# The last two tiles of the second block: values first, gates by halves of the tokens, each half with a norm and store of its own

## The reference

```
gate = sigmoid(h @ w_ple_gate)        # 1024 -> 1024
h    = h + gate * (p @ w_ple_proj)    # 256  -> 1024, per-layer embedding
y    = h * rsqrt(mean(h*h, axis=-1) + 1e-6) * g_final
return y                              # 512 x 1024, f32
```

## Time and profile before

| | us |
|---|---|
| three timed runs | 2205.54, 2205.90, 2208.24 |
| median | 2205.9 |
| the profiled execution | 2205.49 |
| its span in the trace | 2203.5 |
| mean granted clock of PE, share of full speed | 0.993 |

### The profile page before, as it was taken

How to read it: one execution, slowest core, us unless ns; L and a number is a source line. 1 busy time by engine, 2 the same in 40 slices (tenths; PEclk the granted TensorE clock), 3 DMA queues, 4 the chain that set the end, 5 groups by cost and what they waited for, 6 DMA issues and landing times.

```text
span 2203.5 us, 33251 instructions
## 1 busy us (share of the span) xinstructions
PE 2167.4 (98%) x13078; PEld 1830.8 (83%) x13078; DVE 1099.0 (50%) x1711; ACT 822.7 (37%) x1397; POOL 890.8 (40%) x404
## 2 busy tenths in 40 slices
PE   8999999999999999999999999999999999999997
PEld 7987799999999867888888878888878788887876
DVE  5568655642642276540143369656664554443224
ACT  3348734313433375442233322244433332222233
POOL 2322643433443454444444433333334444444443
PEclk9999999999999999999999999999999999999999
DMA  5620045324343701333333374233223243332331
GB/s 147 171 65 2 2 131 155 89 77 129 93 127 93 204 6 39 88 94 95 95 96 90 91 170 140 83 94 84 82 81 96 77 115 95 95 95 82 93 93 67
DMA packets 374985, 210.59 MB, mean 96 GB/s; under 512 B 26399, under 2 KB 367488, under 8 KB 373968
## 3 DMA queue, kind: packets, MB, share of 16 engines
q1 hardware_dynamic: 364454, 191.94, 30.8%
q10 hardware_dynamic: 10410, 16.94, 2.8%
HBM read 196.82 MB, written 15.40 MB: 96 GB/s over the span
## 4 chain that ended last, share of the span: by engine, by line
issue 45%; PE 31%; POOL 21%; DVE 1%; ACT 1%; POOLq 0%; DMA 0%; ACTq 0%; DVEq 0%
POOL w_lo L836 20%; PE acc L974 7%; PE acc L975 7%; PE acc L976 7%; PE acc L1059 2%; PE ops L1100 2%; PE tps L1084 2%; PE ops L1098 1%; PE ops L1082 1%; PE tps L1034 0%; DVE probs L2271 0%; POOL probs L865 0%; POOLq L835 0%; PE acc L1127 0%; ACT sq_x L1698 0%
## 5 line engine op out<-in xcount | busy, mean ns | idle before, releaser
L836 POOL TENSOR_TENSOR w_lo<-raw,w_hi 128x1024 fp32r<-128x1024 f32 x328 | 799.5, 2438 | 1172.7 <-ACT w_hi L1503 1162.9
L1503 ACT ACTIVATE w_hi<-raw 128x1024 fp32r<-128x1024 f32 x327 | 346.3, 1059 | 1039.5 <-PE acc L976 1027.9
L974 PE MATMUL acc<-hr_hi,w_hi 128*128 128x512 f32 x1120 | 447.3, 399 | 1.2 <-DVE qkv L2875 0.6
L976 PE MATMUL acc<-hr_hi,w_lo 128*128 128x512 f32 x1120 | 443.0, 396 | 0.0
L975 PE MATMUL acc<-hr_lo,w_hi 128*128 128x512 f32 x1120 | 442.9, 395 | 0.0
L974 PE MATMUL acc<-hn_hi,w_hi 128*128 128x264 f32 (+1 forms) x872 | 257.7, 295 | 5.3 <-DVE hn_lo L2357 5.1
L974 PEld LDWEIGHTS acc<-hr_hi,w_hi 128*128 128x128 f32 x1120 | 210.5, 188 | 54.4 <-issue 3.7
L975 PE MATMUL acc<-hn_lo,w_hi 128*128 128x264 f32 (+1 forms) x872 | 254.1, 291 | 0.0
L976 PE MATMUL acc<-hn_hi,w_lo 128*128 128x264 f32 (+1 forms) x872 | 254.0, 291 | 0.0
L976 PEld LDWEIGHTS acc<-hr_hi,w_lo 128*128 128x128 f32 x1120 | 210.4, 188 | 50.8
L975 PEld LDWEIGHTS acc<-hr_lo,w_hi 128*128 128x128 f32 x1120 | 210.5, 188 | 49.9 <-issue 0.7
(11 more groups left out here) (435 smaller groups left out, 3689.7 us busy)
## 6 DMA issues: line engine op xcount, KB each, us to landing
raw<-in_w_up SPq DMA_DIRECT2D x64, 512.0 KB, 4.0
raw<-in_w_down SPq DMA_DIRECT2D x64, 512.0 KB, 4.1
raw<-in_w_in SPq DMA_DIRECT2D x56, 512.0 KB, 3.9
raw<-in_w_ffn_gate SPq DMA_DIRECT2D x22, 512.0 KB, 3.8
raw<-in_w_ffn_up SPq DMA_DIRECT2D x22, 512.0 KB, 3.7
raw<-in_w_in_even SPq DMA_DIRECT2D x18, 512.0 KB, 5.8
raw<-in_w_ffn_down SPq DMA_DIRECT2D x16, 512.0 KB, 4.1
raw<-in_w_in_odd SPq DMA_DIRECT2D x10, 512.0 KB, 5.6
```

What stands on the lines that cost most here:

```text
L836: nc.gpsimd.tensor_tensor(w_lo[:, part], raw[:, slot], w_hi[:, part].bitcast(F32), ALU.subtract).then_inc(sems["lo"], T.up("lo"))
L974: mm(out, w_hi[:, part, w0 + k, :], xh, start=s0, stop=False)
L976: ins = mm(out, w_lo[:, part, w0 + k, :], xh, start=False, stop=s1)
L1503: fn(w_hi[:, n % 2], raw[:, n % 4], ACT.Copy).then_inc(sems["hi"], T.up("hi"))
```

## The change

`ple` keeps three steps (tiles 0 to 5). Two new projections follow: `ple_values` (one unit of values for tiles 6 and 7, which ACT copies into `hid_2`) and `ple_gates` (two units, tiles 6 and 7). The gates are run by hand as four pieces of 24 matmuls with 256 tokens each, in the order (tile 6, tokens 0 to 255), then the transposes of tiles 4 and 5, (tile 7, first half), (tile 6, second half), then transposes and norm sums of the first half, (tile 7, second half), and the same for the second half. The halves lie in different PSUM banks.

```
     ple = Projection("ple", [...],
-                     DT // 2, DT // 2, peel=1, order=list(range(0, DT, 2)))
+                     DT // 2 - 1, DT // 2 - 1, peel=1, order=list(range(0, DT - 2, 2)))
+    ple_values = Projection("ple_values", [[(w_ple_proj, 0, 0, 2, "p", w_ple_proj[:, :, P:])], []], 1, 1, order=[DT - 2])
+    ple_gates = Projection("ple_gates", [[(w_ple_gate, 0, 0, 8, "hn2")], [(w_ple_gate, P, 0, 8, "hn2")]], 1, 1,
+                           order=[DT - 2])
+        TOKENS = SEQ // 2
+        def tokens(n):
+            return slice(TOKENS * n, TOKENS * n + TOKENS)
 # SP
             units(ple)
+            units(ple_values)
+            units(ple_gates)
 # PE
+            project(ple_values)
+            gates = []
+            def gate_half(x, n):
+                if n == 0:
+                    gates.append((next_weights(), open_()))
+                part, b = gates[x]
+                for k in range(DT):
+                    ins = three(acc[b][:, n, 0:TOKENS], part, k, hr_hi[:, k, tokens(n)], hr_lo[:, k, tokens(n)],
+                                k == 0, k == DT - 1)
+                ins.then_inc(sems["gate_full"], T.up("gate_full"))
+            def turn_last(n):
+                T.saw("result_last", 2)
+                pe.wait_ge(sems["result_last"], T.at("result_last"))
+                transposes("t_", [...4 blocks of out_t, tiles 6 and 7, two rows of tokens...])
+                T.saw("last_square", 2)
+                pe.wait_ge(sems["last_square"], T.at("last_square"))
+                b = open_("o_")
+                for q in range(2):
+                    c = slice(P * (2 * n + q), P * (2 * n + q) + P)
+                    for i, x in enumerate((sumsq, sq[:, 0, :], sq[:, 1, :])):
+                        ins = mm(ops_[b][:, q:q + 1], x[:, c], ones[:, 0:1], start=i == 0, stop=i == 2)
+                close(ins, b, "o_")
+            gate_half(0, 0)
+            turn_result(DT - 4)
+            turn_result(DT - 3)
+            gate_half(1, 0)
+            gate_half(0, 1)
+            T.saw("sumsq", DT - 1)
             pe.wait_ge(sems["sumsq"], T.at("sumsq"))
+            turn_last(0)
+            gate_half(1, 1)
+            turn_last(1)
 # ACT
             project(ple, embed, own=(0, 1))
+            def keep_values(m, s, t, b):
+                act.wait_ge(sems[f"full{b}"], T.at(f"full{b}"))
+                if t:
+                    next_hi(False)
+                fn(hid_2[:, 1, t, :], acc2[b], ACT.Copy).then_inc(sems[f"stored{b}"], T.up(f"stored{b}"))
+            project(ple_values, keep_values, own=(0, 1))
+            def gate_half(x, n): ...       # Sigmoid, 256 tokens, into hid_2
+            def squares_of_last(x, n): ... # waits "gated", Square, 256 tokens, into sq
+            def root(n): ...               # waits the sums, Sqrt of 2 columns into rstd_tok
+            def store_even(n):
+                q = 2 * n
+                T.saw("rstd_tok")
+                act.wait_ge(sems["rstd_tok"], T.at("rstd_tok"))
+                done = out_sb[:, q, 0:6 * P]
+                fn(done, done, ACT.Copy, scale=rstd_tok[:, q:q + 1]).then_inc(sems["out_act"], T.up("out_act"))
+                act.wait_ge(sems["out_act"], T.at("out_act"))
+                T.saw("out_part")
+                act.wait_ge(sems["out_part"], T.at("out_part"))
+                dma(out[q * P:(q + 1) * P, :], out_sb[:, q, :], "done")
+            gate_half(0, 0)
+            gate_half(1, 0)
+            squares_of_last(0, 0)
+            squares_of_last(1, 0)
+            gate_half(0, 1)
+            fn(small[:, 6:7], eps, ACT.Sqrt).then_inc(sems["metas"], T.up("metas"))
+            root(0)
+            fn(small[:, 7:8], eps, ACT.Sigmoid).then_inc(sems["metas"], T.up("metas"))
+            gate_half(1, 1)
+            fn(small[:, 5:6], eps, ACT.Sqrt).then_inc(sems["metas"], T.up("metas"))
+            store_even(0)
+            squares_of_last(0, 1)
+            squares_of_last(1, 1)
+            root(1)
+            store_even(1)
 # DVE
             project(ple, embed, own=(0, 1))
+            project(ple_values, lambda *_: None, own=(0, 1))
+            keep_result(DT - 4)
+            keep_result(DT - 3)
+            def gate_half(x, n): ...  # values * gate, h + that, times the gain into out_t; 256 tokens each
+            def scale_rows(n): ...    # reciprocal of 2 columns; the 256 new columns of both rows of
+                                      # tokens scaled out of PSUM; the other 768 columns of the odd row
+            gate_half(0, 0)
+            gate_half(1, 0)
+            gate_half(0, 1)
+            scale_rows(0)
+            gate_half(1, 1)
+            scale_rows(1)
```

More of the change, by code:

```diff
@@ L1465, in _ @@
             project(ple, None, H_LO, after_tile=ple_tile)
-            turn_result(DT - 2)
-            turn_result(DT - 1)
-            T.saw("sumsq", DT + 1)
+            project(ple_values)
[11 more added lines that the diff above has]
+                pe.wait_ge(sems["result_last"], T.at("result_last"))
+                transposes("t_", [(lambda t, q=q, x=x: t[:, 256 * q + P * x:256 * q + P * x + P],
+                                   out_t[:, DT - 2 + x, P * (2 * n + q):P * (2 * n + q) + P], 0)
+                                  for q in range(2) for x in range(2)])
+                T.saw("last_square", 2)
[12 more added lines that the diff above has]
+            T.saw("sumsq", DT - 1)
             pe.wait_ge(sems["sumsq"], T.at("sumsq"))
[L1470 to L1473, removed]
+            turn_last(0)
+            gate_half(1, 1)
+            turn_last(1)
         @block.scalar
@@ new lines, in _, with gate_half, squares_of_last @@
+            project(ple_values, keep_values, own=(0, 1))
+            banks = [take(T, "") for _ in range(2)]
+            def gate_half(x, n):
+                T.saw("gate_full")
+                act.wait_ge(sems["gate_full"], T.at("gate_full"))
+                fn(hid_2[:, x, 2, tokens(n)], acc[banks[x]][:, n, 0:TOKENS], ACT.Sigmoid).then_inc(
+                    sems["gate"], T.up("gate"))
+            def squares_of_last(x, n):
+                T.saw("gated")
+                act.wait_ge(sems["gated"], T.at("gated"))
+                if n == 0:
+                    act.wait_ge(sems["sumsq"], T.at("sumsq"))
+                fn(sq[:, x, tokens(n)], h[:, DT - 2 + x, tokens(n)], ACT.Square).then_inc(
+                    sems["last_square"], T.up("last_square"))
@@ new lines, in root @@
+            def root(n):
+                b = result(T, "o_")
+                act.wait_ge(sems[f"o_full{b}"], T.at(f"o_full{b}"))
+                fn(rstd_tok[:, 2 * n:2 * n + 2], ops_[b][:, 0:2], ACT.Sqrt, bias=eps, scale=1.0 / D_MODEL).then_inc(
+                    sems[f"o_stored{b}"], T.up(f"o_stored{b}"))
+            def store_even(n):
[4 more added lines that the diff above has]
+                fn(done, done, ACT.Copy, scale=rstd_tok[:, q:q + 1]).then_inc(sems["out_act"], T.up("out_act"))
@@ new lines, in _, with gate_half @@
+            keep_result(DT - 4)
+            keep_result(DT - 3)
+            def gate_half(x, n):
+                T.saw("gate")
+                dve.wait_ge(sems["gate"], T.at("gate"))
+                G, hm, k = hid_2[:, 1, x, tokens(n)], h[:, DT - 2 + x, tokens(n)], DT - 2 + x
+                step(v.tensor_tensor(G, G, hid_2[:, x, 2, tokens(n)], ALU.mult))
+                v.tensor_tensor(hm, hm, G, ALU.add).then_inc(sems["gated"], T.up("gated"))
+                dve.wait_ge(sems["gated"], T.at("gated"))
+                v.tensor_scalar(out_t[:, k, tokens(n)], hm, gains[:, 56 + k:57 + k], None, ALU.mult).then_inc(
+                    sems["result_last"], T.up("result_last"))
@@ new lines, in scale_rows @@
+            def scale_rows(n):
+                o, b = others(T, "o_"), result(T, "t_")
+                dve.wait_ge(sems[f"o_stored{o}"], T.at(f"o_stored{o}"))
+                x = rstd_tok[:, 2 * n:2 * n + 2]
+                v.reciprocal(x, x).then_inc(sems["rstd_tok"], T.up("rstd_tok"))
+                dve.wait_ge(sems["rstd_tok"], T.at("rstd_tok"))
+                dve.wait_ge(sems[f"t_full{b}"], T.at(f"t_full{b}"))
+                q = 2 * n
+                v.tensor_scalar(out_sb[:, q, 6 * P:], tps[b][:, 0:256], rstd_tok[:, q:q + 1], None, ALU.mult).then_inc(
+                    sems["out_part"], T.up("out_part"))
+                q += 1
+                v.tensor_scalar(out_sb[:, q, 6 * P:], tps[b][:, 256:512], rstd_tok[:, q:q + 1], None, ALU.mult).then_inc(
+                    sems[f"t_stored{b}"], T.up(f"t_stored{b}"))
+                done = out_sb[:, q, 0:6 * P]
+                v.tensor_scalar(done, done, rstd_tok[:, q:q + 1], None, ALU.mult).then_inc(
+                    sems["out_dve"], T.up("out_dve"))
```

44 lines of the change are left out of this document (8 added, 36 removed).

## The result

| | before | after |
|---|---|---|
| median, us | 2205.85 (11 runs, 2200.95 to 2209.56) | 2212.04 (11 runs, 2207.01 to 2217.95) |
| the profiled execution | 2205.49 | 2212.02 |
| its span in the trace | 2203.5 | 2210.0 |
| ratio to before, 95% interval | | 1.0031 [1.0019, 1.0043] |

The changed kernel is slower by 0.31%, 6.2 us in the medians, where 2213.0 was predicted. The same kernel run once more in a later comparison gave 2212.18 against 2204.39, ratio 1.0031 [1.0017, 1.0045].

A forecast was written before the change was run, and what follows sets the result against it. The prediction took PE, busy 98% of the span, to bound the kernel, with a serial tail behind it. Against the profiled 2205.5, 5.1 + 1.9 + 2.5 - 2.0 = +7.5 gave 2213.0 us, range 2209.5 to 2217.

The forecast's parts named there:

- sign of being wrong: PE's gap ahead of the first 256-column matmul under 2 us, or last gate starting within 3 us of last values' old place.
- The wait: PE, between values 6/7 and the first gate: idle for late-rounded weights and the accumulator, 5.1 us.
- The part put down to the accumulator: PE ahead of values 7: waits until DVE frees the accumulator of values 5, 1.0 us.
- The clock: First gates after PE's gap: the granted clock falls for about 3.9 us, costing +1.9, bounds 0 and some 9.
- the clock holds: Rival at the first gates: no clock fall through the gap, 2213.0 - 1.9 = 2211.1; chance 0.18.
- It falls again between the gates: Rival: a second clock fall at the transposes and one-column sums there slows the last 24 matmuls and 12 passes; 2216.0, chance 0.12.
- The norm between the gates: PE ahead of the last gate piece: the first half's transposes and one-column sums add +2.5 us.
- The tail: After the last product: sigmoid, table load, squares, sums, scaling and store take 12.1 against 14.2, so -2.0 us.
- The order on ACT: In the tail: scaling and storing the first half before the second half's squares costs some 2.8 us.
- Drain at a table change: Rival on ACT: each table change also drains it by another load's length, 1.28 in the tail; 2214.3, chance 0.04.
- Halves of a gate: PE's gates: 96 matmuls of 256 columns instead of 48 of 512, no cost, with 0.3 us either way.
- Not slower: weights in time: Rival at ACT's list after tile 4's gain: early rounding avoids stall and clock fall; 2206.0, chance 0.08.

The follow-up runs named there:

- e1: The changed kernel with ACT rounding the weights of tile 6's gate before tile 5's square and gain; ratio to before 1.0013.
- e2: The changed kernel with 16 unneeded matmuls of 512 columns filling PE's gap ahead of the first gate piece; ratio to before 1.0022.
- e3: The changed kernel with ACT taking the second half's squares before scaling and storing the first half's even rows; ratio to before 1.0033.
- e6: The changed kernel with both ACT reorderings, those of e1 and e3; ratio to before 1.0007.
- e5: The changed kernel with all four gate pieces ahead of both norms, one table load, second half's squares before the first half's store; ratio to before 1.0019.
- e7: The changed kernel with values of tiles 4 to 7 as one unit of weights, then four gate pieces, both norms last; ratio to before 0.9996.
- e9: The kernel of e7 with ACT's rounding of the next unit also moved ahead of tile 3's duty; 2201.58 against 2204.39, ratio 0.9986.
- e8: The changed kernel with e1's earlier rounding and e5's norms behind all gate pieces; ratio to before 1.0001.
- e4: The changed kernel with values still first, but whole gates of 512 tokens and one norm as before; 2214.74, ratio to before 1.0048.

## Why the prediction was right, step by step

The verdict, the mechanism and the time (2213.0, measured 2212.04) hold. By terms, with the first trace's own sizes, +7.5 was forecast and +5.9 came from values 6 to the end. That the time is nearer than the terms is luck: 0.6 of the 6.5 in that trace is the earlier offset, which nothing in the forecast stands for. Neither sign of being wrong came: the gap was 3.71 and not under 2, and the last piece of gate starts at 2195.57, 7.6 after before's values of tile 7 (2187.97).

- **The wait, 5.1: 5.0.** Every date was late by the 0.6 of the earlier offset, and otherwise in place: rounding forecast at 2178.75, seen at 2179.34; `w_lo` at 2182.4, PE's start at 2182.86. e1 moves that one instruction and takes 2.4 away. The part put down to the accumulator, 1.0, was 1.05 counted in slots (2176.44 to 2177.49), 0.81 by the bracket.
- **The clock, 1.9: 1.6**, and 2.4 in the second trace. That it would fall was right, and e2 shows the gap as its cause; it came inside the gap in one trace and 0.8 after it in the other. Of the rivals, *the clock holds* is out in both. *It falls again between the gates* is out too: 1.00 through that norm in every trace that has one there (after twice, e1, e2, e3, e6). What none of the cases held is that it can fall again in the tail alone: 1.2 us in the second trace, e1 and e2, 0 in the first trace and e3.
- **The norm between the gates, 2.5: 1.7** (2193.88 to 2195.57). A pass of one column was taken at 0.17, from 8 passes in 1.35. But those passes of before ran partly at the lower level, as the stretch of before around them shows, with a granted clock of 0.72 (it wasn't read for the prediction). At the full clock a pass is 0.11.

```profile
2193.90:2195.30 1.40, 1.33 (x8) 1.25 (x8) 1.15 (x2) 0.02 (x1) 0.00 (x0) 0.72 0.00 0
```

  This is the term that was mis-sized most; its lower bound, 1.9, was too high as well.
- **The tail, -2.0: -2.7.** Of the 0.7, 0.5 is the same error: 12 passes in 1.54 from their start to the root, forecast 2.05. The other 0.2 lies in the sum itself: 14.2 - 12.1 is 2.1, and 12.1 counts from the last matmul's start where 14.2 counts from its slot's end. The order on ACT that was said to cost 2.8 did so in part: e3 gives back 1.4 of it, since beside the squares PE's own transposes and their wait set the date. The last store took 4.4 from its issue at 2205.61, forecast 4.5.
- **Drain at a table change.** After each of three loads the next activation starts at its end: 2199.09 + 1.28 = 2200.37, next 2200.38. The Trainium skill (ScalarE: Activation LUTs, What ACT_TABLE_LOAD costs) adds a drain of about 1380 ns; no load here shows it, so the trace disagrees. The Trainium skill's advice (ScalarE: Activation LUTs, Table sets: the hidden batching unit) to finish one set before the next goes with e5, which has one load and is faster, but no run shows the loads as the reason: the place of the squares and of the norm make up e5's gain, and two of the three loads lay beside PE's work.
- **Halves of a gate**, taken at nothing, cost 0.3: 24 matmuls of 256 columns 2.85, where half of 5.6 is 2.8, and a start of 0.1 after the sums.
- **Not slower: weights in time.** The place that it named was the right one: with the rounding moved (e1) 2.7 of the 5.9 us go by the traces, 2.8 of 6.2 by the medians. Its full price, 7.0, no run of the changed kernel shows, since e1 leaves waits of 0.81 and 1.30. That even a rounding straight after tile 4's gain would come too late is what e1 shows: 1.30 of wait left. Only a longer stretch of values (e7, e9) removes it.

Open: what decides the clock of the last sums. With 1.78 and 1.52 of waiting ahead of them they ran at the lower level in three traces of four (the second of after, e1, e2, not the first of after); with 1.78 and 0.16 at 1.00 in one of two (e3; in e6 the stretch has 0.60), and with both norms last, where the waits ahead of them are 0.16 or none, at 1.00 in all four (e5, e7, e8, e9). So less waiting goes with the full clock, but single traces don't make a rule, and e3 and e6 have the same waits. Before and e4, whose one norm stands there, have 0.72 and 0.67. And how much of e9's gain over e7 is there in the median stays open too.

## What to carry to other kernels

When a short unit of work is moved ahead of a long one, the staging of the next unit no longer has the long one's time to hide in: count, for every unit, from when its first staging step can be issued (behind which duties of that engine's list?) to when PE wants it. A list written by loops changes its order at the boundary between two loops; look there first, here one misplaced rounding was worth 2.4 us and 1.5 more by the clock. And let a stage that waits for other engines (a norm) stand in a time in which PE has to wait anyway, not between its dense work; here that was worth 0.8 to 0.9 us, and the order of ACT's squares ahead of the last sums 1.4.

## What the runs showed of the hardware

- The date at which the granted clock falls isn't fixed by the gap: after a wait of 3.71 us it fell once 0.8 us after work had begun again and once before it, in two executions of one program with the same wait to 0.01 us. Waits of 0.81 and 1.30 left it at 1.00 (e1, e6, e8), one of 2.09 in e7 was followed by a fall.
- Passes of one column go with PE's clock as dense work does: 12 of them take 1.5 us at the full level and 2.7 at the lower one.
- GpSimd's subtraction of a 128x1024 unit takes 2.4 us alone, 2.64 with DVE at work, and two in a row 4.68, so nothing is lost between them.
- Where half of the output is still to be stored (1.05 MB, in after and the same in e1, e3 and e6) the span ends 4.4 us after the last store's issue. Where all four rows of 128 tokens are (2.1 MB) it ends 5.1 us after it in e5, e7 and e8, and 6.8 (2192.26 to 2199.1) in e9, the same program end as e7's: there the rate was 400 GB/s up to 2196.4 and 25 for 2.0 us after it, and why is open.
